# Four gated networks on one core: tile pairs in seven 256-column block products, the down product in three rounds

## The chip, the cores and the metric

The kernel runs on one core of a Trainium2 chip. The metric is the device time of one execution in microseconds (us), as the median of several executions. TensorE (PE) multiplies and writes PSUM; VectorE (DVE) and ScalarE (ACT) read PSUM and SBUF; GpSimd (POOL) reads and writes SBUF alone; SyncE (SP) issues the transfers of weights. Each engine works through its own queue in order and waits on semaphores that the others raise.

## The reference, cut to what matters

Two model blocks are computed for 512 tokens of width 1024 in float32. The part that the change touches is a gated network, which stands four times in the second block (two layers, a first and a second one in each):

```
def rmsnorm_2(x, gain):
    y = x32 * lax.rsqrt(jnp.mean(x32 * x32, axis=-1, keepdims=True) + EPS)
    return (y * gain)
def swiglu(h, w_gate, w_up, w_down):
    return (jax.nn.silu(h @ w_gate) * (h @ w_up)) @ w_down
x = x + 0.5 * swiglu(rmsnorm_2(x, norm), w_gate, w_up, w_down)
```

`w_gate` and `w_up` are 1024 by 2816, `w_down` is 2816 by 1024. Between the networks lie a pooling mixer and a latent attention mixer, and ahead of all four a first block with attention, memory attention and a convolutional network.

## The kernel before, in words

Everything is held transposed: a tile has 128 channels on the partitions and the 512 tokens in the columns. `x` is 8 such tiles. Every weight matrix is cut into units of 128 by 128 pieces: a unit of the gate or up product is one output tile, 8 pieces deep (1024 columns of SBUF, 512 KB); the down product takes three units (8, 8 and 6 pieces) for each of its 8 output tiles.

Float32 precision is kept with two numbers of a shorter type in the place of one. For each weight unit SP fetches it (`fetch`, into one of 3 `raw` buffers), ScalarE makes the high part (`high`, L370, `wh`), VectorE the low part (`low`, L378, `wl`). The activations have a high and a low part too (`hxh`, `hxl` from `split_high` and `split_low`, `hh` and `hl` for the down product). One piece is three matmuls (`mm3`, L386 to L388): high by high, high by low, low by high. `linear` runs one unit, 8 pieces or 24 matmuls of 512 columns.

The four networks are called f10, f20, f11 and f21. Each runs `swiglu_tensor`, `swiglu_scalar`, `swiglu_vector` and `swiglu_gpsimd`, whose order is written out by hand. For each of the 22 tile pairs TensorE computes the gate tile and the up tile into two PSUM banks. VectorE scales both by the inverse root of the mean square (`rs`, L1647 and L1652), ScalarE applies silu (L1637), GpSimd multiplies the two (L1703), ScalarE makes the high part `hh` (L1640), GpSimd the low part `hl` (L1705). The first pair is computed together, step by step (`linear_pair`). The sum of squares of `x` is taken by one-column matmuls (`square_sums`) after the gate tile of pair 1; VectorE makes the mean square from it (`mean_square`, L477), GpSimd the inverse root (`inverse_root`, L484), TensorE spreads it over the rows (`spread_rows`, L494) after the up tile of pair 1, ScalarE keeps it (`keep_rows`, L501). For f10 the two TensorE steps come one tile later (the list `LATE`). Then come the 8 down tiles, 66 matmuls each, and VectorE adds each to `x` (L1692).

A `high` may only overwrite a `wh` buffer when the unit three before has been used by TensorE, so weights are prepared at most three units ahead. All waits go through counting semaphores: `sig.up` raises one and gives names to the count, `sig.at` is what a reader waits for. A `Ring` hands out buffers in turn, and the one who takes a buffer waits for its last reader.

Of the kernel before, what the change touches and what calls it, by code (L numbers as in the profile page):

```python
# [25 lines left out]
NCONV = 3  # L26
CONV_K = 31
PAD = 15
NEG = -1.0e30


def weight_units():
# [24 lines left out]

    ffn("w_up", 0, "w_up", DFF, "w_down")
    for i in range(2):
        ffn(f"f1g{i}", 0, f"f1u{i}", 0, f"f1d{i}")  # L60
# [13 lines left out]
        ffn(f"f2g{i}", 0, f"f2u{i}", 0, f"f2d{i}")  # L74
    return u

# [132 lines left out]
def f(ap):  # L209
    return ap.bitcast(F32)  # L210


def build(nc, wts, xT, memT, pos, cols, ident_d, perm_d, rope_d, pool_d, mask_d, out):
    with ExitStack() as ctx:
        sig = Signals(nc, ctx)
        Ring.made.clear()
        units = weight_units()
        unit_no = {}
# [3 lines left out]
        for _, _, nk, _, w in units:  # L222
            offsets.append(off)
            off += P * nk * w
# [25 lines left out]
        wh = [new("wh", [P, SLOT], F32R) for _ in range(NCONV)]  # L250
        wl = [new("wl", [P, SLOT], F32R) for _ in range(NCONV)]
# [61 lines left out]
        Map.top = base  # L313
        band = new("band", [P, 4, 3, P])
# [31 lines left out]

        def weights_of(i):
            nk, w = units[i][2], units[i][4]
            h = wh[i % NCONV][:, 0:nk * w].rearrange("p (k m) -> p k m", k=nk)
            lo = wl[i % NCONV][:, 0:nk * w].rearrange("p (k m) -> p k m", k=nk)  # L350
            return h, lo

        def fetch(e, i):
            if i >= len(units):
                return
            n = units[i][2] * units[i][4]
            src = wts[offsets[i]:offsets[i] + P * n].rearrange("(p n) -> p n", n=n)
            if i >= NRAW:
                e.wait_ge(*sig.at(("low", i - NRAW)))
            e.dma_start(raw[i % NRAW][:, 0:n], src).then_inc(*sig.up(f"fetched{i % NRAW}", ("fetched", i), by=16))  # L360

        def high(e, i):
            if i >= len(units) or i <= done_to["high"]:
                return
            done_to["high"] = i
            n = units[i][2] * units[i][4]
            e.wait_ge(*sig.at(("fetched", i)))
            if i >= NCONV:
                e.wait_ge(*sig.at(("unit", i - NCONV)))
            e.activation(wh[i % NCONV][:, 0:n], raw[i % NRAW][:, 0:n], ACT.Copy).then_inc(*sig.up("weight_high", ("high", i)))  # L370

        def low(e, i):
            if i >= len(units) or i <= done_to["low"]:
                return
            done_to["low"] = i
            n = units[i][2] * units[i][4]
            e.wait_ge(*sig.at(("high", i)))
            e.tensor_tensor(wl[i % NCONV][:, 0:n], raw[i % NRAW][:, 0:n], f(wh[i % NCONV][:, 0:n]), ALU.subtract) \  # L378
                .then_inc(*sig.up("weight_low", ("low", i)))

        done_to = {"high": -1, "low": -1}
# [1220 lines left out]
        half_turn = Ring(tmp_slots)  # L1602

        def swiglu_tensor(e, nm, u):
            if nm == "f11":
                wide.pass_over(3)
            for c in range(FT):
                g, old_g = wide.take((nm, "gate", c))
                p, old_p = wide.take((nm, "up", c))
                e.wait_ge(*sig.at(old_g))  # L1610
                if c == 0:
                    e.wait_ge(*sig.at(old_p))
                    linear_pair(e, u, g[:, :], p[:, :], normed(nm))
                else:
                    linear(e, u + 2 * c, g[:, :], normed(nm))
                    if c == 1 and nm not in LATE:
                        square_sums(e, nm, KC - 1)
                    if c == 2 and nm in LATE:
                        spread_rows(e, nm, ("root", nm))
                    e.wait_ge(*sig.at(old_p))  # L1620
                    linear(e, u + 2 * c + 1, p[:, :], normed(nm))
                    if c == 1 and nm in LATE:
                        square_sums(e, nm, KC - 1)
                    elif c == 1:
                        spread_rows(e, nm, ("root", nm))
            if nm == "f21":
                mainb.pass_over(1)
            for m in range(KC):
                b, old = mainb.take(("y", nm, m))
                e.wait_ge(*sig.at(old))  # L1630
                for p in range(3):
                    linear(e, u + 2 * FT + 3 * m + p, b[:, :], h_src(nm), 8 * p, p == 0, p == 2)

        def gated_scalar(e, nm, c, ended):
            s = half_turn.of((nm, "gs", c))
            e.wait_ge(*sig.at(("gate", nm, c)))
            e.activation(s[:, :], s[:, :], ACT.Silu).then_inc(*sig.up("silu", ("silu", nm, c)))  # L1637
            e.wait_ge(*sig.at(("joined", nm, c)))
            e.wait_ge(*sig.at(ended))
            e.activation(hh[:, c, :], s[:, :], ACT.Copy).then_inc(*sig.up("h_high", ("hh", nm, c)))  # L1640

        def gated_vector(e, nm, u, c):
            s1, old = half_turn.take((nm, "gs", c))
            e.wait_ge(*sig.at(("rs", nm)))
            e.wait_ge(*sig.at(("unit", u + 2 * c)))
            e.wait_ge(*sig.at(old))
            e.tensor_tensor(s1[:, :], wide.of((nm, "gate", c))[:, :], rs[:, :], ALU.mult) \  # L1647
                .then_inc(*sig.up("half_scaled", ("gate", nm, c), ("free", (nm, "gate", c))))
            s2, old = half_turn.take((nm, "us", c))
            e.wait_ge(*sig.at(("unit", u + 2 * c + 1)))  # L1650
            e.wait_ge(*sig.at(old))
            e.tensor_tensor(s2[:, :], wide.of((nm, "up", c))[:, :], rs[:, :], ALU.mult) \  # L1652
                .then_inc(*sig.up("half_scaled", ("up", nm, c), ("free", (nm, "up", c)), *([("free", ("rs", nm))] if c == FT - 1 else [])))

        def swiglu_scalar(e, nm, u, ended, next_nm, next_gain):
            for i in range(1, 4):
                high(e, u + i)
            for c in range(1, FT):
                high(e, u + 2 * c + 2)
                if c == 1:  # L1660
                    high(e, u + 5)
                    if nm in LATE:
                        high(e, u + 6)
                    keep_rows(e, nm)
                    gated_scalar(e, nm, 0, ended)
                high(e, u + 2 * c + 3)
                gated_scalar(e, nm, c, ended)
            for m in range(KC):
                for p in range(3):
                    high(e, u + 2 * FT + 3 * m + p + 2)  # L1670
                if next_nm:
                    split_high(e, next_nm, m, next_gain, ("x", nm, m))

        def swiglu_vector(e, nm, u, next_nm, next_gain):
            for i in range(1, 4):
                low(e, u + i)
            low(e, u + 4)
            if nm in LATE:
                low(e, u + 5)
            mean_square(e, nm, 1.0 / D)  # L1680
# [1145 lines left out]
```

## Time and profile before

| | |
|---|---|
| median of 3 runs | 2551.04 us (2550.62 to 2552.26) |
| profiled execution, its span | 2550.8 us |
| TensorE busy | 2514.7 us, 99% of the span |
| TensorE weight loads busy | 2073.3 us, 81% |
| VectorE busy | 1215.6 us, 48% |
| ScalarE busy | 933.4 us, 37% |
| GpSimd busy | 622.4 us, 24% |
| one of the networks, f11, from its first matmul to its last addition to `x` | about 361 us |

Busy times are sums of instruction durations, and matmuls overlap in the record, so what counts for TensorE is the distance from one start to the next. A row of the timeline gives the start, the duration, the engine, the line, what is written from what, and in brackets how long the engine had been idle and what released it. The span and the median differ by 0.2 us.

### The profile page before, as it was taken

Reading aid. Unit: us, or ns where it says so; the run is one execution under the profiler, and the core shown is the slowest. Engines: PE = TensorE matmul, PEld = TensorE weight load, DVE = VectorE, ACT = ScalarE, POOL = GpSimd, SP = SyncE. Lnnn points to the kernel's source line nnn. Section 1 sums busy time; section 2 is a strip of 40 time slices with the busy share of each in tenths; the row PEclk is TensorE's granted clock in tenths of the full one; section 3 lists DMA queues with packets and bytes.
Section 4 is the critical chain, followed back from the end, with each engine's and each line's share of the span. In section 5 each row is a group of like instructions: output and inputs, shape, how many; then the busy total and the mean of one; then the engine's idle time right before and its main releaser. Section 6 shows DMA issues by size and latency. Waiting matters only on the chain.

```text
span 2550.8 us, 28691 instructions
## 1 busy us (share of the span) xinstructions
PE 2514.7 (99%) x11642; PEld 2073.3 (81%) x11642; DVE 1215.6 (48%) x1607; ACT 933.4 (37%) x1371; POOL 622.4 (24%) x477
## 2 busy tenths in 40 slices
PE   8999999999999999999999999999999999999999
PEld 7777777888887888888888888888888888888887
DVE  5896655565635333335333333333336566433322
ACT  4486443444323332224333222332223554433221
POOL 3673403222203222101222101222101431322200
PEclk9999999999999999999999999999999999999999
DMA  5211312323232233332323332323332111333232
GB/s 171 71 46 58 105 44 67 107 92 98 93 99 81 90 93 98 98 97 75 107 92 96 96 99 88 108 93 97 92 100 87 42 50 58 94 96 95 93 99 93
DMA packets 66483, 227.26 MB, mean 89 GB/s; under 512 B 7216, under 2 KB 8752, under 8 KB 66352
## 3 DMA queue, kind: packets, MB, share of 16 engines
q1 hardware_dynamic: 66352, 225.44, 28.1%
q8 instruction: 92, 1.51, 0.3%
q14 instruction: 39, 0.32, 0.0%
HBM read 223.31 MB, written 2.10 MB: 88 GB/s over the span
## 4 chain that ended last, share of the span: by engine, by line
PE 89%; DVE 6%; ACT 2%; issue 1%; POOL 1%; DMA 0%; SPq 0%; DVEq 0%; ACTq 0%; POOLq 0%
PE main L386 19%; PE main L388 19%; PE main L387 19%; PE score L386 7%; PE score L388 6%; PE score L387 6%; PE out L386 3%; PE out L388 3%; PE out L387 3%; DVE wl L378 1%; DVE hxl L523 1%; DVE tmp L1347 1%; PE main L2055 1%; ACT wh L370 0%; PE turn L1027 0%
## 5 line engine op out<-in xcount | busy, mean ns | idle before, releaser
L378 DVE TENSOR_TENSOR wl<-raw,wh 128x1024 fp32r<-128x1024 f32 (+1 forms) x431 | 562.8, 1308 | 806.9 <-ACT wh L370 805.9
L370 ACT ACTIVATE wh<-raw 128x1024 fp32r<-128x1024 f32 (+1 forms) x431 | 439.9, 1024 | 635.7 <-PE main L388 473.2
L386 PE MATMUL main<-hxh,wh 128*128 128x512 f32 x1200 | 470.9, 392 | 8.2 <-DVE tmp L687 4.2
L388 PE MATMUL main<-hxh,wl 128*128 128x512 f32 x1200 | 467.9, 390 | 0.0
L387 PE MATMUL main<-hxl,wh 128*128 128x512 f32 x1200 | 467.8, 390 | 0.0
L386 PE MATMUL main<-hh,wh 128*128 128x512 f32 x880 | 342.4, 389 | 0.5 <-DVE wl L378 0.5
L387 PE MATMUL main<-hl,wh 128*128 128x512 f32 x880 | 342.3, 389 | 0.0
L388 PE MATMUL main<-hh,wl 128*128 128x512 f32 x880 | 342.3, 389 | 0.0
L452 POOL TENSOR_TENSOR acc<-acc,sq 128x512 f32<-128x512 f32 (+1 forms) x88 | 128.2, 1456 | 617.4 <-ACT sq L447 612.1
L386 PEld LDWEIGHTS main<-hxh,wh 128*128 128x128 f32 x1200 | 225.7, 188 | 60.1 <-DVE tmp L687 4.3
L388 PEld LDWEIGHTS main<-hxh,wl 128*128 128x128 f32 x1200 | 225.7, 188 | 47.5
L387 PEld LDWEIGHTS main<-hxl,wh 128*128 128x128 f32 x1200 | 225.7, 188 | 45.7
L1703 POOL TENSOR_TENSOR tmp<-tmp,tmp 128x512 f32<-128x512 f32 x88 | 113.5, 1289 | 607.7 <-DVE tmp L1652 562.8
L386 PE MATMUL score<-hxh,wh 128*128 128x512 f32 x656 | 257.3, 392 | 3.0 <-DVE wl L378 1.3
L388 PE MATMUL score<-hxh,wl 128*128 128x512 f32 x656 | 255.4, 389 | 0.0
L387 PE MATMUL score<-hxl,wh 128*128 128x512 f32 x656 | 255.3, 389 | 0.0
L386 PEld LDWEIGHTS main<-hh,wh 128*128 128x128 f32 x880 | 165.2, 188 | 35.0 <-issue 0.9
L387 PEld LDWEIGHTS main<-hl,wh 128*128 128x128 f32 x880 | 165.2, 188 | 34.4
L388 PEld LDWEIGHTS main<-hh,wl 128*128 128x128 f32 x880 | 165.2, 188 | 34.2
L1640 ACT ACTIVATE hh<-tmp 128x512 fp32r<-128x512 f32 x88 | 55.7, 633 | 317.8 <-POOL tmp L1703 317.8
L386 PEld LDWEIGHTS score<-hxh,wh 128*128 128x128 f32 x656 | 123.2, 188 | 32.3 <-DVE hxl L523 4.0
L388 PEld LDWEIGHTS score<-hxh,wl 128*128 128x128 f32 x656 | 123.1, 188 | 25.9
(434 smaller groups left out, 3412.5 us busy)
## 6 DMA issues: line engine op xcount, KB each, us to landing
raw<-in_wts SPq DMA_DIRECT2D x375, 512.0 KB, 3.5
raw<-in_wts SPq DMA_DIRECT2D x52, 384.0 KB, 3.0
x<-in_xT SPq DMA_DIRECT2D x4, 512.0 KB, 8.3
out<-x SPq DMA_DIRECT2D x8, 256.0 KB, 3.2
memx<-in_memT SPq DMA_DIRECT2D x1, 1024.0 KB, 9.6
raw<-in_wts SPq DMA_DIRECT2D x4, 256.0 KB, 2.6
band<-in_pool SPq DMA_DIRECT2D x1, 768.0 KB, 4.2
rope<-in_rope SPq DMA_DIRECT2D x1, 512.0 KB, 7.1
```

The costliest lines, as they stand in the source:

```text
L370: e.activation(wh[i % NCONV][:, 0:n], raw[i % NRAW][:, 0:n], ACT.Copy).then_inc(*sig.up("weight_high", ("high", i)))
L378: e.tensor_tensor(wl[i % NCONV][:, 0:n], raw[i % NRAW][:, 0:n], f(wh[i % NCONV][:, 0:n]), ALU.subtract) \
L386: e.matmul(o, ah, bh, start=start, stop=False)
L387: e.matmul(o, ah, bl, start=False, stop=False)
L388: return e.matmul(o, al, bh, start=False, stop=stop)
L452: e.tensor_tensor(acc[:, 0:n], acc[:, 0:n], sq_turn(nm).of(("sq", nm, k))[:, 0:n], ALU.add) \
L523: e.scalar_tensor_tensor(hxl[:, k, :], x[:, k, :], col(gain, k), f(hxh[:, k, :]), ALU.mult, ALU.subtract) \
L1347: e.scalar_tensor_tensor(s[:, :], y[:, m, :], col(gain, m), turnb.of(("rows", nm))[:, :], ALU.mult, ALU.mult) \
L1640: e.activation(hh[:, c, :], s[:, :], ACT.Copy).then_inc(*sig.up("h_high", ("hh", nm, c)))
L1703: e.tensor_tensor(s1[:, :], s1[:, :], s2[:, :], ALU.mult).then_inc(*sig.up("h_joined", ("joined", nm, c), ("free", (nm, "us", c))))
L2055: made = e.matmul(o[:, n * i:n * i + n], s[:, i * P:(i + 1) * P], ones[:, 2:4] if halves else ones[:, 0:1], start=True, stop=True)
```

## The change

It concerns the four networks alone. Seven of the 22 tile pairs of each (0, 1, 2, 5, 10, 13, 18) are computed as before, 512 columns wide; 5, 10, 13 and 18 have their units cut in two halves of four pieces. The other 15 pairs are computed from seven block products. The two output tiles (up and gate), the two halves of the depth and the two halves of the tokens (`LEFT`, `RIGHT`, 256 columns) form 2 by 2 blocks. Each product is 4 pieces deep, three matmuls a piece, 12 matmuls of 256 columns; so a pair takes 84 matmuls of 256 columns where it took 48 of 512.

What this adds for each of the 15 pairs: four sums of weight halves on VectorE (`sum_step`: S1 is the sum of the gate unit's halves, S2 is S1 less the upper half of the up unit, S3 and S4 are differences), seven high and seven low parts of 512 columns in place of two of 1024, three copies of a PSUM block by ScalarE (`keep_scalar`), since one bank is carried on through four of the products, and three additions and two scalings of 256 columns on VectorE. Once for each network the activations get four sums of their blocks (`turned_sums_vector`, into `tsum`), with their own high and low parts (`th`, `tl`).

GpSimd no longer multiplies gate and up or makes the low parts; VectorE does both. A pair of the plain kind has its up tile multiplied straight out of PSUM, without `rs`, which is applied after the down product instead. The down product runs in three rounds (pairs 0 to 7, 8 to 15, 16 to 21), each with all 8 output tiles; each tile of each round is scaled into a buffer and added to `x`, so there are 24 scalings and 24 additions in the place of 8 fused ones. The first two tiles of a round are interleaved with the last two block products. Inside the networks there are four `raw` and four `wh` and `wl` buffers in place of three, in halves; weights are prepared up to 6 halves ahead, sums up to 9. Outside the networks the units, their order and the three buffers are as before.

```
+ROUNDS_OF = ((0, 8), (8, 8), (16, 6))
+OPENING = 3
+HALVED = (5, 10, 13, 18)
+def tile_order(rnd):
+    for c in range(c0, c0 + n):
+        if c < OPENING:
+            order += [(c, GATE), (c, UP)]
+        elif c in HALVED:
+            order += [(c, GATE_TOP), *behind[:1], (c, GATE_LOW), *behind[1:], (c, UP_TOP), (c, UP_LOW)]
+            behind = []
+        else:
+            order += [(c, UP_LEFT), (c, UP_RIGHT), *behind[:1], (c, S2), *behind[1:], (c, S1), (c, S3)]
+            behind = [(c, GATE_RIGHT), (c, S4)]
+    return order + behind
...
+        a_banks, c_banks, b_banks = Ring(banks[0:2]), Ring(banks[2:4]), Ring([banks[4], banks[7]])
...
+        def block_product(e, nm, c, which):
...
+            for k in range(4):
+                mh, ml, ready = moving(nm, which, k)
+                e.wait_ge(*sig.at(ready))
+                e.matmul(b[:, LEFT], h[:, k, :], mh, start=first and k == 0, stop=False, skip_group_check=not first)
+                e.matmul(b[:, LEFT], h[:, k, :], ml, start=False, stop=False, skip_group_check=not first)
+                made = e.matmul(b[:, LEFT], lo[:, k, :], mh, start=False, stop=k == 3, skip_group_check=not first)
...
+        def keep_scalar(e, nm, c, which):
+            t, old = kept_turn.take((nm, "kept", c, which))
+            e.wait_ge(*sig.at(old))
+            e.wait_ge(*sig.at(("unit", part_no[(nm, c), which])))
+            e.activation(t[:, :], a_banks.of((nm, "a", c))[:, LEFT], ACT.Copy).then_inc(*sig.up("sum_kept", ("kept", nm, c, which)))
...
+        def block_scalar(e, nm, ended, next_nm, next_gain):
...
+                    if which1 in (UP_LEFT, S2, S3):
+                        keep_scalar(e, nm, c1, which1)
+                    if which:
+                        weights_ahead(high, e, part_of(nm, c, which))
+                    if rnd == 0 and s == 0:
+                        for k in range(4):
+                            left_copy_scalar(e, nm, k)
+                        turned_high_scalar(e, nm, 0)
...
+        def block_vector(e, nm, next_nm, next_gain):
...
+                    if which:
+                        weights_ahead(sum_weights, e, part_of(nm, c, which), AHEAD + 3)
+                        weights_ahead(low, e, part_of(nm, c, which))
+                    if rnd == 0 and s == 0:
+                        turned_sums_vector(e, nm, 0)
+                        turned_sums_vector(e, nm, 1)
+                        turned_low_vector(e, nm, 0)
+                    if rnd == 0 and s == (3 if nm in LATE else 2):
+                        mean_square(e, nm, 1.0 / D)
...
+                    if rnd == 0 and s == 5:
+                        gate_plain_vector(e, nm, 0)
+                        gate_plain_vector(e, nm, 1)
...
+                    e.scalar_tensor_tensor(y[:, :], down_banks.of((nm, "bank", rnd, m))[:, :], 0.5, rs[:, :], ALU.mult, ALU.mult) \
...
+                    e.tensor_tensor(x[:, m, :], x[:, m, :], y[:, :], ALU.add) \
...
-            for c in range(FT):
-                s1, s2 = half_turn.of((nm, "gs", c)), half_turn.of((nm, "us", c))
-                e.wait_ge(*sig.at(("silu", nm, c)))
-                e.wait_ge(*sig.at(("up", nm, c)))
-                e.tensor_tensor(s1[:, :], s1[:, :], s2[:, :], ALU.mult).then_inc(*sig.up("h_joined", ("joined", nm, c), ("free", (nm, "us", c))))
-                e.wait_ge(*sig.at(("hh", nm, c)))
-                e.tensor_tensor(hl[:, c, :], s1[:, :], f(hh[:, c, :]), ALU.subtract).then_inc(*sig.up("h_low", ("h", nm, c), ("free", (nm, "gs", c))))
```

The first place at which the change shows in the queues is VectorE at the opening of f20, from the low part of the unit of gate tile 1 on. In the names, `tsum` holds the block sums of the activations, `th` and `tl` their high and low parts, `sum` the sums of weights; the brackets give the semaphores that an instruction waits for. Before:

```order
L378 TENSOR_TENSOR wl_63<-raw_57,wh_60 128x1024 [waits s_weight_high]
L378 TENSOR_TENSOR wl_61<-raw_55,wh_58 128x1024 [waits s_weight_high]
L477 TENSOR_SCALAR stat_79<-turn 128x4 [waits s_sums_done]
L378 TENSOR_TENSOR wl_62<-raw_56,wh_59 128x1024 [waits s_weight_high]
L1647 TENSOR_TENSOR tmp_78<-score,rs_69 128x512 [waits s_h_joined,s_unit_done,s_rows_kept]
```

Now, from the first of the activation sums on:

```order
L1943 SCALAR_TENSOR_TENSOR tsum_146<-x_49,colsb_64,tsum_146 128x256 [waits s_left_kept]
L1946 SCALAR_TENSOR_TENSOR tsum_146<-x_49,colsb_64,tsum_146 128x256 [waits s_turned_sum]
L1949 TENSOR_TENSOR tsum_146<-tsum_146 128x256 [waits s_turned_sum]
L1950 SCALAR_TENSOR_TENSOR tsum_146<-x_49,colsb_64,tsum_146 128x256
...
L1955 TENSOR_TENSOR tl_145<-tsum_146,th_144 128x1024 [waits s_turned_high]
L526 TENSOR_TENSOR wl_63<-raw_57,wh_60 128x1024 [waits s_weight_high]
L552 TENSOR_TENSOR sum_135<-raw_57 128x512 [waits s_fetched2,s_unit_done,s_fetched1,s_weight_low]
L552 TENSOR_TENSOR sum_136<-sum_135,raw_56 128x512 [waits s_weights_summed,s_weight_low]
L526 TENSOR_TENSOR wl_61<-raw_55,wh_58 128x1024 [waits s_weight_high]
L670 TENSOR_SCALAR stat_79<-turn 128x4 [waits s_sums_done]
```

The mean square (L477, now L670) stood three instructions behind the low part of a unit; now two rounds of activation sums, a `tl`, two low parts and two weight sums lie ahead of it, and the first weight sum reads the buffer `raw_57` that the low part just ahead of it has only then released.

The second place is ScalarE in a run of two block pairs of f20, where the silu of one pair and the copies for the next stand in one queue. Before:

```order
L370 ACTIVATE wh_59<-raw_56 128x1024 [waits s_unit_done,s_fetched1]
L370 ACTIVATE wh_60<-raw_57 128x1024 [waits s_unit_done,s_fetched2]
L1637 ACTIVATE tmp_74<-tmp_74 128x512 [waits s_half_scaled]
L1640 ACTIVATE hh_121<-tmp_74 128x512 [waits s_h_joined]
```

Now:

```order
L1961 ACTIVATE kept_129<-main 128x256 [waits s_unit_done]
L517 ACTIVATE wh_142<-raw_57 128x512 [waits s_fetched2]
L517 ACTIVATE wh_142<-raw_55 128x512 [waits s_fetched0]
L517 ACTIVATE wh_58<-raw_57 128x512 [waits s_unit_done]
L1966 ACTIVATE tmp_78<-tmp_78 128x512 [waits s_block_made]
L1961 ACTIVATE kept_130<-main 128x256 [waits s_unit_done]
L517 ACTIVATE wh_58<-sum_136 128x512 [waits s_weights_summed]
L517 ACTIVATE wh_59<-raw_56 128x512 [waits s_fetched1]
L517 ACTIVATE wh_59<-raw_56 128x512 [waits s_unit_done]
L1971 ACTIVATE bh_127<-tmp_78 128x512 [waits s_blocks_joined]
```

The copy `kept_130`, for which TensorE waits before it goes on in that bank, now stands behind a silu (L1966) that waits for VectorE.

## Rows read from the trace of the kernel before

**Rows 1.** The page: the span, busy times, and engines on the chain of waits.

```profile
span 2550.8 us, 28691 instructions
...
PE 2514.7 (99%) x11642; PEld 2073.3 (81%) x11642; DVE 1215.6 (48%) x1607; ACT 933.4 (37%) x1371; POOL 622.4 (24%) x477
...
PE 89%; DVE 6%; ACT 2%; issue 1%; POOL 1%; DMA 0%; SPq 0%; DVEq 0%; ACTq 0%; POOLq 0%
```

**Rows 2.** Timeline of VectorE, end of f11: start, duration, instruction, idle before.

```profile
1904.24 0.69 DVE L1692 SCALAR_TENSOR_TENSOR x<-main,x 128x512 f32<-128x512 f32 x1 [1.70 <-PE main L388]
1919.20 0.69 DVE L1692 SCALAR_TENSOR_TENSOR x<-main,x 128x512 f32<-128x512 f32 x1 [1.70 <-PE main L388]
```

**Rows 3.** Timeline of TensorE, pooling mixer: matmuls of 1 and of 256 columns.

```profile
1169.73 0.35 PE L469 MATMUL turn<-ones,acc 128*128 128x1 f32 x2 [0.72 <-ACT sq L447]
...
1172.21 0.41 PE L387 MATMUL main<-wl,hxh 128*128 128x256 f32 x1
1172.42 0.41 PE L388 MATMUL main<-wh,hxl 128*128 128x256 f32 x1
...
1178.09 0.28 PE L388 MATMUL score<-wh,hxl 128*128 128x256 f32 x1
...
1181.68 0.28 PE L388 MATMUL out<-wh,hxl 128*128 128x256 f32 x1
```

**Rows 4.** Groups of VectorE by form: busy us, mean ns of one, idle before.

```profile
L378 DVE TENSOR_TENSOR wl<-raw,wh 128x512 fp32r<-128x512 f32 x4 | 2.8, 690 | 6.7 <-ACT wh L370 6.7
L2363 DVE TENSOR_TENSOR pt<-turn,pt 128x256 fp32r<-128x256 f32 x8 | 3.4, 419 | 3.0 <-ACT pt L2358 3.0
L1778 DVE SCALAR_TENSOR_TENSOR zl<-main,stat,zh 128x256 fp32r<-128x256 f32 x8 | 3.7, 479 | 1.9 <-ACT zh L1767 1.6
```

**Rows 5.** Timeline of VectorE, opening of f20.

```profile
1209.64 2.36 DVE L378 TENSOR_TENSOR wl<-raw,wh 128x1024 fp32r<-128x1024 f32 x2 [1.36 <-ACT wh L370]
...
1222.67 0.68 DVE L1652 TENSOR_TENSOR tmp<-out,rs 128x512 f32<-128x512 f32 x1
1223.27 0.68 DVE L1647 TENSOR_TENSOR tmp<-main,rs 128x512 f32<-128x512 f32 x1
```

**Rows 6.** Groups of ScalarE and of GpSimd by form.

```profile
L370 ACT ACTIVATE wh<-raw 128x512 fp32r<-128x512 f32 x4 | 2.5, 625 | 7.6 <-PE main L388 7.6
L2358 ACT ACTIVATE pt<-turn 128x256 fp32r<-128x256 f32 x8 | 3.0, 374 | 4.3 <-PE turn L2351 4.3
L1703 POOL TENSOR_TENSOR tmp<-tmp,tmp 128x512 f32<-128x512 f32 x88 | 113.5, 1289 | 607.7 <-DVE tmp L1652 562.8 <-ACT tmp L1637 45.0
```

**Rows 7.** Timeline of ScalarE, VectorE, GpSimd and TensorE, opening of f20.

```profile
1208.55 2.01 ACT L370 ACTIVATE wh<-raw 128x1024 fp32r<-128x1024 f32 x2 [2.38 <-PE score L388]
...
1215.65 1.02 POOL L484 TENSOR_TENSOR stat<-stat,mhalf 128x4 f32<-128x4 f32 x1 [8.45 <-DVE stat L477]
...
1220.80 0.60 PE L494 MATMUL turn<-ident,stat 128*128 128x128 f32 x4
```

**Rows 8.** The page, DMA issues of a whole unit: KB each, median us to landing.

```profile
raw<-in_wts SPq DMA_DIRECT2D x375, 512.0 KB, 3.5
```

**Rows 9.** Timeline, opening of f10: ScalarE, VectorE, GpSimd, TensorE.

```profile
816.29 2.01 ACT L370 ACTIVATE wh<-raw 128x1024 fp32r<-128x1024 f32 x2 [1.14 <-PE score L388]
...
815.19 6.69 DVE L378 TENSOR_TENSOR wl<-raw,wh 128x1024 fp32r<-128x1024 f32 x3
...
814.77 12.05 POOL L452 TENSOR_TENSOR acc<-acc,sq 128x512 f32<-128x512 f32 x6
...
834.92 0.60 PE L494 MATMUL turn<-ident,stat 128*128 128x128 f32 x4
```

**Rows 10.** Timeline of TensorE, a long gap early in the kernel.

```profile
61.51 0.56 PE L386 MATMUL main<-hxh,wh 128*128 128x512 f32 x1 [4.21 <-DVE tmp L687]
61.86 0.63 PE L387 MATMUL main<-hxl,wh 128*128 128x512 f32 x1
62.29 0.63 PE L388 MATMUL main<-hxh,wl 128*128 128x512 f32 x1
```

More of the change, by code:

```diff
@@ L25 @@
 NRAW = 3
-NCONV = 3
+NHALF = 6
+HALF = 512
+AHEAD = 6
+Q = 256
 CONV_K = 31
@@ L29 @@
 NEG = -1.0e30
+ROUNDS_OF = ((0, 8), (8, 8), (16, 6))
+BLOCKED = ("f10", "f20", "f11", "f21")
+OPENING = 3
+HALVED = (5, 10, 13, 18)
+UP_LEFT, UP_RIGHT, S4, GATE_RIGHT, S1, S2, S3 = 1, 2, 3, 4, 5, 6, 7
+GATE_TOP, GATE_LOW, UP_TOP, UP_LOW = 8, 9, 10, 11
+GATE, UP = 12, 13
+SUMS = (S1, S2, S3, S4)
+def tile_order(rnd):
+    c0, n = ROUNDS_OF[rnd]
+    order, behind = [], []
+    for c in range(c0, c0 + n):
[8 more added lines that the diff above has]
+    return order + behind
 def weight_units():
@@ new lines, in build, with raw_half @@
+        area_ready = {"f10": ("unit", unit_no["f1g0"][0] - 1), "f20": ("unit", unit_no["f2g0"][0] - 1),
+                      "f11": ("unit", unit_no["f1g1"][0] - 1), "f21": ("unit", unit_no["mla_out"][0] + 1)}
+        tile_raw = {}
+        for (_, r, tile, _) in parts:
+            if tile:
+                tile_raw[r], tile_raw[r + 1] = (tile, True), (tile, False)
+        sums = Ring(sum_slots)
+        def raw_half(r, half):
+            return raw[raw_slot[r]][:, half * HALF:half * HALF + HALF]
@@ new lines, in weight_source @@
+        def weight_source(i):
+            n, (_, r, tile, which) = units[i][2] * units[i][4], parts[i]
+            if tile is None:
+                return raw[raw_slot[r]][:, 0:n], ("fetched", r)
+            if which in SUMS:
+                return sums.of(("sum", tile, which))[:, :], ("summed", tile, which)
+            gate = which in (GATE_TOP, GATE_LOW, GATE_RIGHT)
+            half = 1 if which in (GATE_LOW, UP_LOW, UP_RIGHT, GATE_RIGHT) else 0
+            return raw_half(r + gate, half), ("fetched", r + gate)
@@ new lines, in sum_weights, with reach, weights_ahead @@
+        def sum_weights(e, i):
+            if i >= len(units):
+                return
+            _, _, tile, which = parts[i]
+            if which == S2:
+                sum_step(e, tile, S1)
+            if which in SUMS:
+                sum_step(e, tile, which)
+        def reach(i, halves):
+            n = i
+            while n + 1 < len(units) and ends[n + 1] <= ends[i] + halves:
+                n += 1
+            return n
+        def weights_ahead(step, e, i, halves=AHEAD):
+            for n in range(i + 1, reach(i, halves) + 1):
+                step(e, n)
@@ L384, in mm3 @@
+        done_to, summed = {"high": -1, "low": -1}, set()
         def mm3(e, o, a, b, start, stop):
```

549 lines of the change are left out of this document (419 added, 130 removed).

## The prediction

> **What bounds the kernel now.** I read the page first: TensorE is busy for 99% of the span and is 89% of the chain of waits, while VectorE has 48%, ScalarE 37% [rows 1]. So the time is the sum of what TensorE issues, and only two things can move it: the distance from one matmul's start to the next, and gaps. The distance at 512 columns comes from the end of f11: the additions to `x` follow each other by 1919.20 - 1904.24 = 14.96 us, and 66 matmuls lie between them, 0.2267 us each with all waits inside [rows 2]. At 256 columns and the full clock, the pooling mixer shows 30 matmuls between 1178.09 and 1181.68, 0.1197 us each, across a change of bank and unit [rows 3]. That is more than half of 0.2267 (0.1133): each matmul carries a share that doesn't shrink with its columns.
>
> **What TensorE saves.** A plain pair is 48 x 0.2267 = 10.88 us, a block pair 84 x 0.1197 = 10.05 us. The gain is 0.83 us, for 15 pairs in 4 networks 60 x 0.825 = **49.5 us**. The down product keeps its 528 matmuls a network. This is 7/8 of the columns, but only 0.924 of the time.
>
> The Trainium skill (TensorE: Matmul & The Clock Gate, Back-to-back issue gap) puts the gap at N/2.4 + 2.5 ns, 109 ns at 256 columns and 216 ns at 512. By that the gain would be 48 x 0.2158 - 84 x 0.1092 = 1.19 us a pair, 71 us in all. Both rows here are some 11 ns above the page, so the rows decide; its result stands below as a rival.
>
> **The runs of block pairs.** VectorE's prices: 0.60 us from start to start at 512 columns (1222.67 to 1223.27), about 1.15 at 1024 (two in 2.36) [rows 5]. At 256 columns a record lasts 0.42 [rows 4]; with the same 0.09 overlap I estimate 0.33. A block pair asks for 13 operations of 512 columns (7 low parts, 4 sums, the product of gate and up, its low part) and 5 of 256: 7.8 + 1.65 = 9.45 us, with some 0.15 for S2 that waits for S1. That fits into 10.05 us with 0.4 to spare. The upper bound takes whole records, 13 x 0.69 + 5 x 0.42 = 11.1 us [rows 4]. I take the lower, since rows 5 are operations issued back to back, as these are. ScalarE needs 9 x 0.54 + 3 x 0.29 = 5.7 us (0.63 and 0.37 less the same overlap) [rows 6], so it has room. GpSimd loses 176 operations of 1.29 us [rows 6]; that work was hidden and saves nothing by itself, but while it ran beside VectorE a unit's low part could double [rows 9], so its going holds VectorE at the lower price. Plain pairs and down tiles ask for less: 7 x 0.6 = 4.2 of 10.88 us, and 1.15 + 0.6 + 0.6 = 2.4 of 5.44.
>
> A product waits for ScalarE's copy of its bank, with two other products (2.87 us) in between, in the first pair of a run one (1.44 us). Copy and semaphores are some 0.6 us. The tight place is the copy of S2 in the second pair of a run. It stands behind the silu of the pair before, which waits for VectorE. Counted from the end of UP_RIGHT, I have VectorE at its addition 1.5 us late (it waits for the copy of S3, then has 0.33 + 0.6 + 0.6 + 1.3 + 0.6 to do), the scaled gate at 3.7, silu at 4.4, the copy at 4.9, and S3 due on TensorE at 4 x 1.436 = 5.7. Slack 0.8 us: no cost. In the down rounds, the last pair's result needs about 2.7 us, behind 30 matmuls (6.8 us) that don't need it. No cost.
>
> **The openings.** Here the change adds what was nowhere before. Count from the first matmul of a network. ScalarE's fourth `high` waits for the first pair: at 1208.55 in f20, so the start is 1197.6, and it ends at 11.8 [rows 7]. The copies of the left columns stand behind it, so nothing of the activation sums starts sooner. Then VectorE has, up to the scaled gate tile 0: 16 operations of 256 columns, whose chain I price at 0.55 + 0.55 + 0.33 + 0.42 = 1.85 us for each of 4 (0.48 a record [rows 4], more where it waits for its own last), 7 operations of 1024 at 1.15, 12 of 512 at 0.6, 0.4 for the rest: 7.4 + 8.05 + 7.2 + 0.4 = 23.05, so it is done at 35.0, and gate tile 2 after four more at 37.4. TensorE ends the three opening pairs at 23.2 (spreading of rows: 1220.80 - 1197.6 [rows 7]) + 0.65 + 10.9 = 34.7. It then needs the bank of gate tile 0, and one product later that of gate tile 2. So f11 stalls 0.3 + 0.9 = **1.2 us**.
>
> In f20 and f21 the first weight sum needs the unit of up tile 3 in the buffer that the low part just ahead (gate tile 2's) releases, as the order shows; f10 and f11 have the fourth buffer for it. The landing takes 3.5 us [rows 8] with VectorE idle. The mean square stands behind: 12 + 7.15 (a low part, two sets of sums, `tl`, a low part) + 3.5 + 1.3 + 1.15 + 0.2 = 25.3, plus GpSimd's 1.02 [rows 7] and semaphores, 26.5, against 23.2: TensorE waits **3.3 us**, then at the banks 0.3 + 1.0, so 4.6 us each.
>
> In f10 GpSimd adds squares from 9.4 to 21.4 us (start 816.2 - 10.88 = 805.4), and beside it a low part took 6.69 / 3 = 2.23 us [rows 9]. From 12 on that halves VectorE's pace for 9.4 us, 4.6 us lost. The mean square stands one step later: 12 + 14.6 + 4.6 + 1.1 = 32.3 against 834.92 - 805.4 = 29.5 [rows 9]: 2.8 us, then 1.2 + 0.9 at the banks: 4.9 us. Sum of the openings: 1.2 + 4.6 + 4.6 + 4.9 = **15.3 us**. From below it could be 0, if the chain is cheaper; from above 25, if each `tl` and chain takes a third more.
>
> **Ends and clock.** The last down tile now takes a scaling and an addition, 0.69 + 0.69 with a semaphore, where it took 0.69: 0.75 us later. The pooling mixer waits for that (0.72 us there already [rows 3]), and so does the end of the kernel: **1.5 us**. After a gap of 4.21 us matmuls of 512 columns started every 0.43 us [rows 10], and after 0.72 us with one-column matmuls those of 256 every 0.21 [rows 3], which is the 1.2 GHz level. Gaps of about 3 us in three openings may do the same; 6 us at half pace costs 3 us, of which the banks' waits come back. I put **3 us** on it (bounds 0 and 9).
>
> **Sum.** 2550.8 - 49.5 + 15.3 + 1.5 + 3 = 2521.1 of span; the median lies 0.2 above the profiled span: **2521 us**.
>
> **Rivals.**
> 1. *The openings hide their work* (sums ahead of the mean square land early, chain cheap): 2551 - 49.5 + 1.5 + 2 = 2505. For it: before the change VectorE idles for most of an opening. Against: the fourth `high` holds everything to 11.8 us. Chance 0.12.
> 2. *The copies cost.* If the handshake misses by 0.2 to 0.4 us in each of 60 pairs, 12 to 24 us: 2533 to 2545. For it: slack of 0.8 us by prices that I partly estimated. Chance 0.17.
> 3. *VectorE binds and the kernel is slower.* If operations don't overlap (11.1 us a pair) and each of four waits costs 0.25 more, a pair takes 12.1 us there. A network has seven runs, six of 2 pairs and one of 3; VectorE falls 2.05 us a pair behind and TensorE tolerates about 2. That costs 4 x (6 x 2.1 + 4.1) = 67 us: 2588. To pass the old time by 0.2% the 28 runs must lose 35 us, 1.25 each, which takes 10.05 + (2 + 1.25) / 2 = 11.7 us a pair on VectorE. Against: rows 5 and 9.45. Chance 0.09, and 0.05 that it ends within 0.2% of the old time.
> 4. *Matmuls at the page's gap*, 71 us gained: 2500. The pooling mixer's own 0.1197 speaks against. Chance 0.02.
>
> **How the numbers follow.** The forecast as worked out (2511 to 2532) has 0.55. The range takes it with rivals 1 and 2 for the most part: 2505 to 2541. A difference under 0.2% (5 us) can't be told from none. Faster: 0.55 + 0.12 + 0.17 + 0.02 = 0.86; same 0.05; slower 0.09.
>
> **What would show it.** Matmuls of 256 columns 0.12 us apart inside the networks; each pair 10.05 us. TensorE idle until the rows are spread in f20, f21 and f10 by about 3 us and not in f11, then about 1 us at the banks of gate tiles 0 and 2. VectorE at over 90% in runs of block pairs, ScalarE near 57%. I am wrong if the block products stand further apart than 0.12, if TensorE waits for `kept` in the runs, or if an opening costs over 8 us.

## The result, and the profile after

The change takes 2575.6 us (median of four runs) where the kernel before takes 2551.7: a ratio of 1.0092, 95% interval 1.0076 to 1.0108. That is 24 us slower, where 30 us faster was forecast. The time is 55 us above the predicted one, and 35 us above the upper end of the range. One of the four, the profiled one, was a disturbed execution of 4918.6 us beside 2573.8 to 2576.3, so the ratio leaves it out, and what is shown as "after" comes from a second measurement of the same kernel (2576.2 us; ratio 1.0090, 1.0073 to 1.0107).

The page of after answers to [rows 1]:

```profile
span 2576.7 us, 34915 instructions
PE 2489.6 (97%) x13802; PEld 2145.5 (83%) x13802; DVE 1731.7 (67%) x2747; ACT 1127.9 (44%) x1915; POOL 393.3 (15%) x301
PE 82%; DVE 10%; ACT 3%; issue 3%; POOL 1%; DMA 1%; SPq 0%; DVEq 0%; ACTq 0%; POOLq 0%
```

TensorE is busy for less of the span than before and is 82% of the chain of waits instead of 89%; VectorE's part of the chain is 10%. So there are new gaps. The waits of TensorE in the same trace say for whom (us in total, times, longest):

```profile
PE turn L687 <- POOL stat L677: 10.2, 3, 4.0
PE main L579 <- DVE tmp L2123: 8.4, 3, 6.4
PE main L579 <- DVE wl L526: 8.3, 10, 3.5
PE main L579 <- DVE x L3039: 7.7, 2, 7.4
PE main L579 <- DVE x L2213: 5.3, 1, 5.3
PE turn L662 <- ACT sq L640: 4.9, 1, 4.9
...
PE main L1853 <- DVE tmp L2017: 2.4, 3, 1.3
```

The first and the last row are the openings, as forecast; two rows of 1.4 and 1.3 for the same `tmp` of L2017 at other banks belong to the last. The other five are not in the prediction, except 1.5 of the 4.9. L2213 and L3039 are the additions to `x` that end the pooling mixer and the attention; L2123 scales a down tile; L526 is a unit's low part.

The saving itself is there. In a run of block pairs the trace of TensorE after reads:

```profile
1004.33 0.28 PE L1853 MATMUL main<-hxh,wh 128*128 128x256 f32 x1
...
1021.60 0.40 PE L579 MATMUL score<-bh,wh 128*128 128x512 f32 x1
```

144 matmuls of 256 columns lie between the two starts: 17.27 / 144 = 0.1199 us each, with every wait, copy and change of bank inside. Over an equal stretch right behind a down round (first row) and over that one (second row) the engines stood so (us, then PE, PEld, DVE, ACT and POOL busy, granted clock, DMA share, GB/s):

```profile
942.13:959.40 17.27, 17.27 (x145) 17.27 (x144) 15.84 (x29) 9.79 (x19) 0.00 (x0) 1.00 0.40 123
1004.33:1021.60 17.27, 17.27 (x145) 17.27 (x144) 13.21 (x23) 9.20 (x17) 0.00 (x0) 1.00 0.41 124
```

VectorE is busy for 92% in the first and for 76% in the second, the least of such stretches, and ScalarE for 57% and 53%; I had expected over 90% and near 57%. TensorE's pace is the same in both. No row of TensorE waits for `kept`. So 55 us are missing elsewhere, and TensorE's waits name three places: the first product of a network, the last down round, and the opening.

### The profile page after: what moved, and what is told of

Its sections match the earlier page's. It is cut to its first block, busy times and chain, and to the rows that moved or that the text cites. A ratio compares the mean times of both kernels' runs of the same rounds, so it can differ in the third digit from the quotient of the medians.

```text
span 4917.3 us, 34915 instructions
## 1 busy us (share of the span) xinstructions
PE 4906.2 (100%) x13802; PEld 3655.9 (74%) x13802; DVE 1738.9 (35%) x2747; ACT 1140.2 (23%) x1915; POOL 382.5 (8%) x301
## 4 chain that ended last, share of the span: by engine, by line
PE 100%; DVE 0%; ACT 0%; issue 0%; DVEq 0%; ACTq 0%
PE main L579 15%; PE main L580 15%; PE main L581 14%; PE score L579 6%; PE main L1855 6%; PE main L1853 6%; PE main L1854 6%; PE score L581 6%; PE score L580 6%; PE out L581 3%; PE out L579 3%; PE out L580 3%; PE score L1855 2%; PE score L1854 2%; PE score L1853 2%; PE main L2482 1%
## 5 line engine op out<-in xcount | busy, mean ns | idle before, releaser
L526 DVE TENSOR_TENSOR wl<-raw,wh 128x512 fp32r<-128x512 f32 (+2 forms) x523 | 511.1, 982 | 900.2 <-ACT wh L517 898.7
L517 ACT ACTIVATE wh<-raw 128x512 fp32r<-128x512 f32 (+2 forms) x523 | 428.9, 829 | 1490.0 <-PE main L581 838.2
L1853 PE MATMUL main<-th,wh 128*128 128x256 f32 x840 | 371.9, 443 | 0.0
L1855 PE MATMUL main<-th,wl 128*128 128x256 f32 x840 | 368.2, 438 | 0.0
L1854 PE MATMUL main<-tl,wh 128*128 128x256 f32 x840 | 366.6, 436 | 0.0
L1854 PEld LDWEIGHTS main<-tl,wh 128*128 128x128 f32 x840 | 295.0, 351 | 5.2 <-issue 5.0
L1853 PEld LDWEIGHTS main<-th,wh 128*128 128x128 f32 x840 | 291.7, 347 | 3.7 <-issue 3.1
L1855 PEld LDWEIGHTS main<-th,wl 128*128 128x128 f32 x840 | 289.5, 345 | 0.1
L579 PE MATMUL main<-bh,wh 128*128 128x512 f32 x352 | 238.0, 676 | 0.0
L580 PE MATMUL main<-bl,wh 128*128 128x512 f32 x352 | 237.5, 675 | 0.0
L526 DVE TENSOR_TENSOR wl<-sum,wh 128x512 fp32r<-128x512 f32 x240 | 162.5, 687 | 124.1 <-ACT wh L517 122.9
```

Of the source, the lines that this page charges most:

```text
L517: e.activation(halves_of(wh, i), src, ACT.Copy).then_inc(*sig.up("weight_high", ("high", i)))
L526: e.tensor_tensor(halves_of(wl, i), src, f(halves_of(wh, i)), ALU.subtract) \
L579: e.matmul(o, ah, bh, start=start, stop=False)
L580: e.matmul(o, ah, bl, start=False, stop=False)
L1853: e.matmul(b[:, LEFT], h[:, k, :], mh, start=first and k == 0, stop=False, skip_group_check=not first)
L1854: e.matmul(b[:, LEFT], h[:, k, :], ml, start=False, stop=False, skip_group_check=not first)
```

## The experiments

Each is told by its difference from the changed kernel where nothing else is said. A saving is the difference of medians. The kernel before had 2551.2 to 2552.9 in the four sets of runs, and the change was measured in another set than the edits, so a saving of 1 or 2 us is not told apart from none.

**The change again**, unedited, for its profile.

> The changed kernel as it is, run again for a profile at full speed (the profiled execution of the first measurement took 4918 us, with matmuls of 512 columns 0.43 us apart nearly everywhere, and can't be laid beside the others). The time should again be 2574 to 2576. Theory A (TensorE's clock): the granted clock of the three other executions was 0.987 against 0.995 before, about 40 us more at half rate, which costs some 20 us; the profile should show stretches of 256-column matmuls 0.21 us apart after gaps in the openings. Theory B (handshakes): TensorE idles 0.3 us or more in each block pair, for copies of ScalarE. Theory C (openings): the four openings cost over 8 us each instead of 4. Theory D (pace): 256-column matmuls of the block products stand further apart than 0.12 us.

2576.2 us, ratio 1.0090 (1.0073 to 1.0107). Theories B and D fall by the stretches above. C holds for f20 and f21, with the waits at their starts counted. A holds in kind, at about half its price (see the clock below).

### A bank that VectorE still reads

The trace after, at the start of f21: TensorE, then VectorE.

```profile
2207.92 0.39 PE L581 MATMUL main<-hxh,wl 128*128 128x512 f32 x1
2215.66 0.79 PE L579 MATMUL main<-hxh,wh 128*128 128x512 f32 x1 [7.35 <-DVE x L3039]
2216.25 0.63 PE L580 MATMUL main<-hxl,wh 128*128 128x512 f32 x1
2216.68 0.63 PE L581 MATMUL main<-hxh,wl 128*128 128x512 f32 x1
```

```profile
2206.94 8.06 DVE L716 SCALAR_TENSOR_TENSOR hxl<-x,colsb,hxh 128x512 fp32r<-128x512 f32 x5 [0.33 <-ACT hxh L708]
2214.93 0.68 DVE L3039 TENSOR_TENSOR x<-main,x 128x512 f32<-128x512 f32 x1
```

The attention's last tile is finished by TensorE at about 2208.3, but the addition that reads its bank stands behind five low parts. The changed kernel gives the first product of f21 that same bank, as `a_banks` and `c_banks` are banks 0 to 3. TensorE waits 7.35 us, and then goes on at half rate, 0.43 us from start to start, until about 2220; the granted clock there is 0.50 of the full one. The starts of f20 (5.33) and f11 (6.37) show the same. The edit gives the first pair banks 4 and 7 instead of the third:

```diff
-            return b_banks if c == OPENING - 1 else a_banks
+            return b_banks if c == 0 else a_banks
...
-            return b_banks if c == OPENING - 1 else c_banks
+            return b_banks if c == 0 else c_banks
```

> The changed kernel, but the first pair of each network, not the third, takes the banks 4 and 7, which no last tile of the stage before is read from. Theory A (bank collision): in the change the first pair of f20, f11 and f21 waits 5.3, 6.4 and 7.4 us until VectorE has read the last tile of the stage before out of the same bank. The three waits go, 19 us, and with them three stretches at half clock after them (some 4 us in all) and about 0.7 us a network at the bank of gate tile 2: 2550 to 2556 us. Rival B (VectorE's own lateness): the wait is only where a late VectorE shows; TensorE then waits as long for the split of the last tile of x or a weight's low part, and the time stays within 5 us of 2576.

2557.4 us (ratio 1.0019, 1.0010 to 1.0029): 18.8 saved, a little less than theory A had. The rows of L2213 and L3039 are gone; at the start of f11 a wait of 4.1 for `wl` L526 takes the place of 6.4 for the bank, so there the bank was only one of two causes.

Was that lateness made by the change? At f20 and f21 it was not. The trace of before, VectorE at the start of f21:

```profile
2185.49 8.19 DVE L523 SCALAR_TENSOR_TENSOR hxl<-x,colsb,hxh 128x512 fp32r<-128x512 f32 x5 [0.33 <-ACT hxh L515]
2193.60 0.68 DVE L2612 TENSOR_TENSOR x<-main,x 128x512 f32<-128x512 f32 x1
```

The addition ends 8 us after TensorE began f21 (2186.0), and nobody waits, because the product ring stands at another bank. At f20 the last addition starts at 1202.72, 4.7 us after TensorE's first product (1198.0). Two edits of the kernel before test this. The first drops the step over three banks at the start of f11:

```diff
-            if nm == "f11":
-                wide.pass_over(3)
```

> The kernel before, with one step undone: its product ring no longer passes over three banks at the start of f11, so that the first products of f11 stand in banks from which VectorE may still read the last tile of f20. Theory A (a first product in a bank whose last reader is VectorE's closing addition waits for it, 5 to 7 us where I saw it in the changed kernel): TensorE waits at the start of f11 for the addition to x, which before came with no wait, and the kernel is 2 to 7 us slower than before, 2554 to 2559. The lower end, because the ring before has five banks and only one or two of them are still being read. Rival B (such a wait needs the changed kernel's heavier VectorE work around it): no new wait, 2551 to 2553.

2554.1 us, ratio 1.0008 (0.9999 to 1.0018): not told apart from none, at the edge of both forecasts. TensorE does wait for the last addition now (0.79 us), but VectorE is idle when that tile's product ends, so the addition follows at once. The second turns the ring at the starts of f20 and f21, where VectorE is late, until it stands at the bank of the last tile:

```diff
+            if nm in ("f20", "f21"):
+                last = wide.of(("pooled", KC - 1)) if nm == "f20" else out_banks.of(("out", KC - 1))
+                while wide.slots[wide.n % 6].t is not last:
+                    wide.pass_over(1)
```

> The kernel before, in which the product ring is turned at the starts of f20 and f21 so that their first product stands in the bank of the last tile of the stage ahead. In the kernel before that tile's addition to x is late already: in f21 it starts at 2193.60, 7.3 us after TensorE began the network at 2186.3, behind five low parts in 8.19 us; in f20 at 1202.72, 5.3 us after 1197.4. Theory A (a bank collision costs as much as VectorE is late, and the lateness was there before the change): TensorE waits about 8.0 us at f21 and 6.1 at f20 and goes on at half rate for some 4 and 3 us, and the kernel is 14 to 18 us slower, 2565 to 2569. Rival B (as where I undid the step over three banks at f11, a collision costs next to nothing in the kernel before): 2551 to 2556.

2569.1 us, ratio 1.0067 (1.0052 to 1.0082), 16.5 us more than before, as theory A had it. Waits of TensorE in it:

```profile
PE main L386 <- DVE x L2616: 7.7, 2, 7.4
PE score L386 <- DVE x L1790: 6.2, 1, 6.2
```

So a collision costs what its reader is late, and at f20 and f21 the lateness is older than the change: taking the collision out of the changed kernel and putting it into the kernel before make that a shown cause. At f11 it is otherwise. VectorE is not late there in the kernel before; it is late in the change because of the last down round, the next section. With that round reordered and the banks as in the change, the 6.37 us at the start of f11 are

```profile
1558.13 0.47 PE L579 MATMUL main<-hxh,wh 128*128 128x512 f32 x1 [0.90 <-DVE tmp L2124]
```

### The last down round

In the third round of the down product each tile has 18 matmuls, 4.08 us. VectorE, f10, after:

```profile
1137.22 0.69 DVE L2123 SCALAR_TENSOR_TENSOR tmp<-score,rs 128x512 f32<-128x512 f32 x1 [2.25 <-PE score L581]
...
1140.68 0.96 DVE L526 TENSOR_TENSOR wl<-raw,wh 128x768 fp32r<-128x768 f32 x1 [0.51 <-ACT wh L517]
1141.56 0.68 DVE L2123 SCALAR_TENSOR_TENSOR tmp<-out,rs 128x512 f32<-128x512 f32 x1
...
1146.41 0.68 DVE L2123 SCALAR_TENSOR_TENSOR tmp<-main,rs 128x512 f32<-128x512 f32 x1
1147.12 0.69 DVE L2126 TENSOR_TENSOR x<-x,tmp 128x512 f32<-128x512 f32 x1
1148.61 0.75 DVE L716 SCALAR_TENSOR_TENSOR hxl<-x,colsb,hxh 128x512 fp32r<-128x512 f32 x1 [0.79 <-ACT hxh L708]
1149.86 1.46 DVE L526 TENSOR_TENSOR wl<-raw,wh 128x768 fp32r<-128x768 f32 x1 [0.50 <-ACT wh L517]
1151.25 0.68 DVE L2123 SCALAR_TENSOR_TENSOR tmp<-main,rs 128x512 f32<-128x512 f32 x1
```

ScalarE beside it:

```profile
1147.85 0.72 ACT L708 ACTIVATE hxh<-x,colsb 128x512 fp32r<-128x512 f32 x1 [2.87 <-DVE x L2126]
1148.48 0.61 ACT L640 ACTIVATE sq<-x 128x512 f32<-128x512 f32 x1
1149.00 0.83 ACT L517 ACTIVATE wh<-raw 128x768 fp32r<-128x768 f32 x1
```

A tile takes 1151.25 - 1146.41 = 4.84 us, 0.76 more than TensorE gives it, and it is a ring: the addition ends (1147.81), ScalarE rounds `x`, squares it and rounds the weights (to 1149.83), VectorE makes their low part, and only behind that starts the next scaling, at 1151.25. VectorE only does 3.6 us of work in it. The kernel before has the same ring in 14.96 us a tile [rows 2].

The first tile of the round went through the same order in 1141.56 - 1137.22 = 4.34 us. Its low part took 0.96 us where the later ones took 1.46, and GpSimd, which adds the square of each later tile (1149.17 to 1150.51 here), did not add then. So 0.26 of the 0.76 us a tile is the order, and 0.50 is the longer low part beside GpSimd; this division is read from the trace, and no run moves GpSimd's additions away. First, in the last round, the weights' low part goes behind the tile's addition, and the low part of the next network's `x` one tile later:

```diff
-                    weights_ahead(sum_weights, e, down_unit(nm, rnd, m), AHEAD)
-                    weights_ahead(low, e, down_unit(nm, rnd, m), 4)
+                    if rnd < 2:
+                        weights_ahead(sum_weights, e, down_unit(nm, rnd, m), AHEAD)
+                        weights_ahead(low, e, down_unit(nm, rnd, m), 4)
...
-                    if rnd == 2 and next_nm:
-                        split_low(e, next_nm, m, next_gain)
+                    if rnd == 2:
+                        weights_ahead(low, e, down_unit(nm, rnd, m), 4)
+                    if rnd == 2 and next_nm and m:
+                        split_low(e, next_nm, m - 1, next_gain)
+                if rnd == 2 and next_nm:
+                    split_low(e, next_nm, KC - 1, next_gain)
```

> The changed kernel, but in the last down round of a network VectorE first scales and adds a tile, then makes the low part of a weight, then the low part of the x tile before it (not of the same one). Theory A (a chain of VectorE and ScalarE of 4.84 us a tile against 4.08 of TensorE): a tile takes 0.76 us too long because VectorE waits 0.8 for the high part of x and 0.5 for that of the weight; reordered it needs some 3.5 us. The five waits of 0.5 us a network go (2 us each in f10, f20, f11), the 4.9 at the pooling mixer falls to about 1.5, the 6.4 at f11 to 1.5 to 2, the 3.5 + 1.3 at the latent mixer to about 0: 18 us, 2555 to 2562. Rival: ScalarE or contention with GpSimd keeps the pace, and the time falls by under 6 us.

2551.7 us (ratio 1.0002, 0.9992 to 1.0012): 24.5 saved, more than theory A's upper end. The edit changes two things at once, so each was made alone. Only the low part of `x` delayed:

> The change with half of the edit of the last down round: the low part of the next network's x is made one tile later, so that it no longer waits for ScalarE's rounding of the same tile; the weights' low part stays ahead of the tile's addition. Theory A (the loop of 4.84 us per tile goes addition, ScalarE's rounding of x and square, ScalarE's rounding of the weights 0.5 us later, weights' low part, addition; the split only lies beside it): the loop keeps its 4.84 us, and the kernel gains 0 to 2 us, 2574 to 2576.5. Rival B (VectorE's own waits of 0.80 and 0.50 make up the tile's time, so that taking out the 0.80 brings it to 4.04, under TensorE's 4.08): nearly the whole gain of the last-round edit, 2552 to 2556.

2573.6 us (ratio 1.0084, 1.0069 to 1.0099), 2.6 less, half a microsecond beyond theory A's range and far from rival B's. VectorE's tile there:

```profile
1146.14 0.74 DVE L716 SCALAR_TENSOR_TENSOR hxl<-x,colsb,hxh 128x512 fp32r<-128x512 f32 x1
1148.27 1.42 DVE L526 TENSOR_TENSOR wl<-raw,wh 128x768 fp32r<-128x768 f32 x1 [1.39 <-ACT wh L517]
```

The wait of 0.79 for `hxh` is gone, and the one for `wh` has grown from 0.50 to 1.39: the ring is 4.79 us. Only the weights' low part moved behind the addition:

> The change with the other half: in the last down round the weights' low part stands behind the tile's addition instead of ahead of it; the low part of the next network's x stays with its own tile. Theory A (the loop through ScalarE's rounding of the weights is cut, since the low part now takes a unit that was rounded a tile earlier): VectorE needs 0.7 + 0.6 + 0.9 + 0.7 us a tile, under TensorE's 4.08, and nearly the whole gain of the last-round edit comes, 2551 to 2556. Rival B (the wait for the rounding of x decides): half of it or less, 2564 to 2575.

2556.8 us (ratio 1.0015, 1.0005 to 1.0024), 19.4 saved, a microsecond short of the expected range. VectorE's tile:

```profile
1148.33 0.69 DVE L2127 TENSOR_TENSOR x<-x,tmp 128x512 f32<-128x512 f32 x1
1148.94 0.95 DVE L526 TENSOR_TENSOR wl<-raw,wh 128x768 fp32r<-128x768 f32 x1
1149.81 0.75 DVE L716 SCALAR_TENSOR_TENSOR hxl<-x,colsb,hxh 128x512 fp32r<-128x512 f32 x1
1151.68 0.69 DVE L2124 SCALAR_TENSOR_TENSOR tmp<-score,rs 128x512 f32<-128x512 f32 x1 [1.12 <-PE score L581]
```

Now VectorE waits for TensorE, 1.12 us in each tile. The low part takes 0.95 us, as it now ends before GpSimd starts. The ring through ScalarE's rounding of the weights was the cause, and cutting it is worth some 20 of the 24.5 us, the shorter low part included.

### The openings

Only the mean square moved ahead of the weight sums in its step:

```diff
+                    if rnd == 0 and s == (3 if nm in LATE else 2):
+                        mean_square(e, nm, 1.0 / D)
                     if which:
...
-                    if rnd == 0 and s == (3 if nm in LATE else 2):
-                        mean_square(e, nm, 1.0 / D)
```

> The changed kernel with the mean square of each network ahead of the weight sums on VectorE. TensorE waits 4.0, 3.4 and 2.9 us for the inverse root in f20, f21 and f10. Theory A (VectorE's queue sets the opening): these waits vanish but come back at the banks of gate tiles 0 and 2, whose scaling stands at the same place in VectorE's queue: the time falls by 0 to 5 us (the 5 by half clock that doesn't happen). Rival (the inverse root sets it): 10 us and the clock's 3, 2562 to 2566.

2575.0 us, ratio 1.0088 (1.0073 to 1.0103): no difference that can be told, as theory A had it. The 10.2 us for `stat` become waits at the banks, one product later:

```profile
PE main L1853 <- DVE tmp L2017: 10.8, 4, 4.1
```

A step that lets TensorE go on earlier gains nothing while VectorE's queue behind it is as long. **All three edits together:**

> The three edits together (free banks, last round reordered, mean square early). Theory: starts and ends of the networks add up, with the overlap at the start of f11 (6.4 us) counted once: 2576 - 19 - 18 + 6 - 10 for the clock and mean square = 2532 to 2542 us, below the kernel before. If the half clock (32 us of matmuls at half rate where before had 12) goes with the gaps, the lower end. Rival: if half or more of the loss is the block products themselves, it stays above 2551.

2534.0 us, ratio 0.9927 (0.9912 to 0.9942). The parts add up: 18.8 + 24.5 + 1.2 = 44.5 singly, 42.2 together. Next, in this version, the scaled gates of tiles 0 and 1 go ahead of the sums and low parts of their step:

```diff
+                    if rnd == 0 and s == 5:
+                        gate_plain_vector(e, nm, 0)
+                        gate_plain_vector(e, nm, 1)
                     if which:
...
-                    if rnd == 0 and s == 5:
-                        gate_plain_vector(e, nm, 0)
-                        gate_plain_vector(e, nm, 1)
```

> The three edits together (free banks, last round, early mean square; 2534.0) and, at the end of an opening, the scaled gates of tiles 0 and 1 placed on VectorE ahead of the sums and low parts of that step instead of behind them. In the three-edit kernel TensorE still waits 11.5 us in 4 times for the bank of gate tile 0 (for tmp L2017). Theory A (the wait is for VectorE's queue: 4 operations of 0.6 us stand ahead of the gate): each wait falls by about 2.4 us, 4 times, 2524 to 2528. Rival B (VectorE only does the same work in another order, and the low parts that are now behind come late for the next product): the wait moves to the weights' low parts, 2531 to 2535.

2525.6 us, ratio 0.9901 (0.9886 to 0.9916): 8.4 saved. And the weight sums of the first three steps one part later, so that VectorE doesn't stand before a unit that is still landing:

```diff
-                        weights_ahead(sum_weights, e, part_of(nm, c, which), AHEAD + 3)
+                        weights_ahead(sum_weights, e, part_of(nm, c, which), AHEAD + (2 if rnd == 0 and s < 3 else 3))
```

> As the early gates, and in the first three steps of an opening the weight sums run one part less ahead, so that VectorE doesn't stand at the first sum of f20 and f21 until its unit has landed, 3.5 us after its buffer came free. Theory A (that landing is what makes the openings of f20 and f21 late): f20 and f21 gain up to 3.5 us each beyond the early gates, f10 and f11 nothing, 2518 to 2525. Rival B (what is asked for later is missing later, since the sums deferred still come before the first block pair): no gain over the early gates, within 1 us of it.

2521.8 us, ratio **0.9886** (0.9870 to 0.9903): 3.8 more, the best version, 29 us faster than the kernel before. By the two traces f20 gives 1.3 us of it and f21 2.5, f11 loses 1.6, and 1.5 lie ahead of f10, where the edit changes nothing. Its page:

```profile
span 2520.8 us, 34919 instructions
PE 2474.5 (98%) x13802; PEld 2139.6 (85%) x13802; DVE 1724.2 (68%) x2747; ACT 1126.3 (45%) x1915; POOL 398.3 (16%) x301
```

Last, the three edits of the openings alone, on the change as made:

> The change as made, with the three edits of the openings alone (mean square earlier, scaled gates earlier, weight sums one part later), the banks and the last down round as in the change. If the openings' waits behind the mean square are separate from those of banks and last round: their 10.2 us for the mean square and 2.4 us for tmp L2017 mostly go, 8 to 12 us faster than the change, 2564 to 2568, with the bank waits of 5 to 7 us at the starts of f20, f11 and f21 still there. If VectorE comes out of the bank collision so late that the opening's chain is bound by it anyway: within 3 us of the change, 2573 to 2576.

2567.2 us, ratio 1.0064 (1.0049 to 1.0079), 9.0 saved. So the openings are a cost of their own, and the smallest of the three.

## Why the prediction was wrong, point by point

- **Block products: right.** 0.1199 us a matmul in the stretch above, against 0.1197 [rows 3]. 84 of them are 10.07 us, so by that pace some 48 of the 49.5 us were saved.
- **VectorE, `kept` and the copies: right.** It keeps up, with 13.2 to 15.8 us of work in 17.3, and the slack of S2 was enough. Rivals 2 and 3 fall, and so does rival 4, whose distance of 0.109 no stretch shows. The kernel became slower without the mechanism of rival 3.
- **Openings: right in their sum.** TensorE waits 2.9, 4.0 and 3.4 us for the mean square in f10, f20 and f21 and not in f11, where I had 2.8, 3.3, 3.3 and none, and 4.9 us at the banks where I had 5.9: 15.1 against 15.3. The parts were less exact: at the banks of f20 I had 1.3 and it was 2.0, at those of f21 0.6. Rival 1 falls.
- **Missed: the first pair's banks.** The prediction followed the banks inside a network (gate tile 0, gate tile 2), and never asked who still reads the bank of the first product; its sum has no term for the start of a network. What it needed was in the trace of before: an addition that ends 8 us after the next stage began. Freeing those banks gave 18.8 us. The test that I had set, an opening over 8 us, was met by this: with the wait at its start the opening of f20 stalls 11.3 us and that of f21 11.4.
- **The step that failed: "No cost" for the down rounds, and "2.4 of 5.44".** 5.44 us is a tile of 24 matmuls, in the first two rounds. In the third a tile has 18, and the splits for the next network fall on it. Even so a sum of durations says that it fits (3.6 of 4.08). What doesn't fit is the ring across two engines with its order, 4.84. Nor did GpSimd's going hold VectorE at the lower price there, as the prediction said: it still adds the squares in this round, and a low part beside it took 1.46 us instead of 0.96. The ring costs 0.76 a tile, then makes VectorE late at the pooling mixer (4.9 instead of 1.5), at the attention and at f11. Undoing it gave 24.5 us.
- **The clock: mechanism right, size too small.** Stretches in which TensorE goes at half its rate (granted 1.2 instead of 2.4 GHz) sum to 11.6 us in the trace of before and 31.7 after, counted from the start of f10. 20 us more at half rate cost about 10, not 3. Each of the new ones follows one of the gaps above, so most of it goes with them: 16.9 us are left in the best version. No run changes the clock alone, so this share is read from the traces and not shown by an edit.
- **Ends: right.** The pooling mixer waits 1.52 us in the version with all three edits where it waited 0.72 [rows 3], and that kernel ends 4.0 us after the start of its last matmul instead of 3.2: 1.6 together, against 1.5.

The ledger: 18.8 (banks) and 24.5 (last round) carry their part of the clock; together with the 1.2 of the mean square and their overlap they explain 42 of the 55 us. The 13 left between 2534.0 and 2521 are partly half rate (21.1 us in that trace, 9.5 more than before, some 5 against the 3 forecast) and waits of 2.0 for `wl` at the start of f11 and of the attention; the rest is spread thin and I have not settled it. That the best version stands at the predicted time is partly chance: it also spends less on the openings than the forecast gave them.

## What to carry to other kernels

When a product stage gets new banks, look up for its first product which instruction last reads that bank and when that instruction runs in the trace of before, not when its product ends. When work per tile is cut into shorter pieces, a loop over two engines that had slack must be walked round in its order, step by step; the sum of busy times on each engine doesn't show it. And move the step that the other engine waits for ahead of the work it doesn't wait for at every place, since one of them alone only moves the wait.

## What the runs showed of the hardware

- The low part of a unit of 768 columns took 1.46 us on VectorE while GpSimd added squares (1149.17 to 1150.51 in the trace after), and 0.95 where it ran apart from it. Five low parts of 512 columns took 8.06 us, 1.6 each, while GpSimd was busy, against 0.75 for one alone. By that difference some 4 of the 7.35 us that TensorE waited at f21 come from it; no run tests this.
- After the wait of 7.35 us matmuls of 512 columns started 0.43 us apart, though TensorE had gone at its full rate until the wait. In the version with all three edits, waits of 3.1 and 4.0 us were also followed by 256-column matmuls at half rate. In the best version a wait of 2.04 us at 1546.04 was followed by 3 us at a granted clock of 0.50, and one of 2.04 us at 1899.40 was not (1.00).
